# A hybrid encoder block on one core: the meta tokens' query steps moved to the front of each differential-attention unit, and the head of the output projection begun inside the last unit

## The reference

```
h    = rmsnorm(x);  proj = h @ w_in            # 3072 columns: NA q,k,v and diff q,k,v
na   = neighbourhood attention, 8 heads of 64
diff = differential attention, 4 heads: softmax(q1 k1) - lam * softmax(q2 k2), times v (128 wide)
diff = rmsnorm(diff over each head's 128) * subln * (1 - lambda_init)
x    = x + concat(na, diff) @ w_out
x    = x + expert_choice_ffn(rmsnorm(x))       # 16 experts, top-k tokens each
y    = rmsnorm(x), meta rows dropped
```

## Time and profile before

| | |
|---|---|
| median of 3 runs | 3216.51 us (3214.36 to 3216.98) |
| the profiled execution | 3214.47 us, of it span 3212.6 us |
| mean granted clock of TensorE | 0.954 |
| TensorE matmuls busy | 2997.2 us, 93% of the span |
| VectorE, ScalarE busy | 1873.7 us (58%), 1480.1 us (46%) |
| GpSimd busy | 170.8 us |

### The profile page before, as it was taken

The page is one execution under the profiler, slowest core; times in us unless marked ns, Lnnn a source line. Parts: engine busy times, 40 slices in busy tenths (PEclk is TensorE's granted clock), DMA queues, the critical chain, the costliest instruction groups (busy, mean ns, idle before and its releaser), DMA issues.

```text
span 3212.6 us, 49879 instructions
## 1 busy us (share of the span) xinstructions
PE 2997.2 (93%) x19549; PEld 2798.3 (87%) x19549; DVE 1873.7 (58%) x2996; ACT 1480.1 (46%) x2506; POOL 170.8 (5%) x177
## 2 busy tenths in 40 slices
PE   7999999898987896799999999999999999999993
PEld 7888887676854775799999999999999999999993
DVE  6232345564755236567667666766766766766672
ACT  4232323333333222456556555655655655555562
POOL 1000000000001000010110100010010011011001
PEclk9999999898988997899999999999999999999996
DMA  5322221100111333577777777777877777777774
GB/s 154 98 68 70 73 62 29 31 27 25 27 60 32 121 124 106 185 229 244 225 234 236 229 232 233 228 238 226 248 224 232 238 229 232 235 229 234 227 224 174
DMA packets 637872, 528.25 MB, mean 164 GB/s; under 512 B 30757, under 2 KB 618663, under 8 KB 637651
## 3 DMA queue, kind: packets, MB, share of 16 engines
q1 hardware_dynamic: 629458, 499.46, 50.1%
q0 software_dynamic: 8192, 25.70, 3.9%
HBM read 472.36 MB, written 40.79 MB: 160 GB/s over the span
## 4 chain that ended last, share of the span: by engine, by line
PE 74%; DVE 4%; ACT 2%; issue 2%; DMA 2%; POOL 1%; SPq 0%; ACTq 0%; POOLq 0%; DVEq 0%
PE ps L1840 38%; PE ps L1841 17%; PE ps L1759 5%; PE ps L1534 5%; PE ps L1729 2%; PE ps L1666 2%; ACT e_df L864 1%; PE ps L1885 1%; PE ps L1709 1%; DVE e_df L1243 1%; PE ps L1834 1%; PE ps L1727 1%; DMA wqkv<-w_in_dram 1%; DVE x L1306 0%; DVE mixT_lo L1293 0%
## 5 line engine op out<-in xcount | busy, mean ns | idle before, releaser
L1840 PE MATMUL ps<-xe,w_hi 128*128 128x392 f32 x4096 | 1196.1, 364 | 1.6 <-DVE xe L1440 1.6
L1841 PE MATMUL ps<-xe,w_lo 128*128 128x196 f32 x4096 | 1034.4, 253 | 0.0
L1427 DVE TENSOR_TENSOR w_lo<-raw,w_hi 128x2048 fp32r<-128x2048 f32 x384 | 875.5, 2284 | 0.2 <-issue 0.2
L1841 PEld LDWEIGHTS ps<-xe,w_lo 128*128 128x128 f32 x4096 | 784.4, 192 | 0.0
L1840 PEld LDWEIGHTS ps<-xe,w_hi 128*128 128x128 f32 x4096 | 770.4, 188 | 1.9 <-DVE xe L1440 1.9
L729 ACT ACTIVATE w_hi<-raw 128x2048 fp32r<-128x2048 f32 x384 | 731.9, 1911 | 10.1 <-DMA raw<-w_down_dram 9.9
L1840 PE MATMUL ps<-hid,w_hi 128*128 128x392 f32 x2048 | 609.4, 366 | 0.0
L1841 PE MATMUL ps<-hid,w_lo 128*128 128x196 f32 x2048 | 516.8, 252 | 0.0
L1841 PEld LDWEIGHTS ps<-hid,w_lo 128*128 128x128 f32 x2048 | 391.4, 191 | 0.0
L1840 PEld LDWEIGHTS ps<-hid,w_hi 128*128 128x128 f32 x2048 | 384.5, 188 | 0.0
L1460 DVE TENSOR_TENSOR gusum<-ps,part 128x392 f32<-128x392 f32 x256 | 145.0, 566 | 396.1 <-ACT part L729 396.1
(11 more groups left out here) (182 smaller groups left out, 3183.8 us busy)
## 6 DMA issues: line engine op xcount, KB each, us to landing
raw<-w_gate_dram SPq DMA_DIRECT2D x128, 1024.0 KB, 5.2
raw<-w_up_dram SPq DMA_DIRECT2D x128, 1024.0 KB, 5.2
raw<-w_down_dram SPq DMA_DIRECT2D x128, 1024.0 KB, 5.3
wqkv<-w_in_dram SPq DMA_DIRECT2D x24, 512.0 KB, 4.4
xt<-x_all_dram SPq DMA_DIRECT2D x12, 512.0 KB, 4.8
v_na<-v SPq DMA_DIRECT2D x64, 96.0 KB, 2.3
mixed_heads<-mix SPq DMA_DIRECT2D x96, 64.0 KB
mixs<-mixed_heads SPq DMA_DIRECT2D x12, 512.0 KB, 5.2
```

Source lines behind the costliest of these rows:

```text
L1427: dve.tensor_tensor(w_lo[:, n % NW, :], raw[:, n % NRAW, :], w_hi[:, n % NW, :].bitcast(f32), ALU.subtract).then_inc(lo_done, 1)
L1840: pe.matmul(out, w_hi[:, slot, cols], x.rearrange("p h n -> p (h n)"), start=first, stop=False)
L1841: return pe.matmul(out[:, 0:SLOTS], w_lo[:, slot, cols], x[:, 0, :], start=False, stop=last)
```

## The change

`diff_steps` now puts the two tail steps first in each unit. After them come the sample tiles and then the prompt tiles in units 0 to 2, and the prompt tiles and then the sample tiles in the last unit. The stores are numbered by step, and the two tail steps share a slot; the second's output waits for the first's square. ScalarE does the square of a step ahead of the exponentials instead of behind the copies.

In the last unit, SyncE issues the loads of T = 0 and T = 1 in steps 8 and 9 (`c_loads` waits by slot for the stores that it needs). VectorE makes the means of the tail tile and of tiles 0 to 3 in step 14 and the scaling of T = 0 and T = 1 in step 15, ahead of the last step's output; GpSimd does the power in three pieces (4, 16 and, after all squares, 32 columns). TensorE waits for all statistics (`df_m`) instead of all outputs before the first transposes of the output projection, and for all outputs before the first `h2_to_columns`. The SBUF places are rearranged so that the early tensors lie over the unused q0, k0 and the projection weights. The clearing of `aff` stays behind the last square.

```diff
-def diff_steps():
-    out = [(t, P, P, 0, PT) for t in range(PT)]
-    out += [(t, P, P, PT, FULL - PT) for t in range(PT, FULL)]
-    out += [(FULL, TAIL, TAIL, PT, FULL - PT), (FULL, TAIL, N_META, 0, PT)]
-    return out
+def diff_steps(last):
+    prompt = [(t, P, P, 0, PT) for t in range(PT)]
+    sample = [(t, P, P, PT, FULL - PT) for t in range(PT, FULL)]
+    tails = [(FULL, TAIL, TAIL, PT, FULL - PT), (FULL, TAIL, N_META, 0, PT)]
+    return tails + (prompt + sample if last else sample + prompt)
...
         mixs = R("mixs", [P, 2, D])
+        assert R.off <= late_off
+        R = Region(after_h)
         mixT_hi = R("mixT_hi", [P, 2, KD, P], f32r)
         mixT_lo = R("mixT_lo", [P, 2, KD, P], f32r)
         xr = R("xr", [P, 2, D])
+        assert R.off <= after_w
+        R = Region(late_off)
         x2 = R("x2", [P, 2, D])
...
-        def df_store(u, t):
-            return NT * UNITS + NT * u + t
+        def df_store(u, n):
+            return NT * UNITS + NT * u + max(n - 1, 0)
+        def stored_before(b, g):
+            return (g - b) // MIXR + 1
+        def last_store(T):
+            return df_store(UNITS - 1, [n for n, x in enumerate(DFS[-1]) if x[0] == c_tile(T)][-1])
...
+            def c_loads(T):
+                b, rows, row = T % 2, c_rows(T), c_tile(T) * P
+                if T >= 2:
+                    sp.wait_ge(mT_ready, T - 1)
+                for slot in range(MIXR):
+                    sp.wait_ge(mix_out[slot], 16 * stored_before(slot, last_store(T)))
+                sp.dma_start(mixs[0:rows, b, :], mix_d[row:row + rows, :]).then_inc(mixs_in[b], 16)
+                if T >= 2:
+                    sp.wait_ge(x2_ready, T - 1)
+                sp.dma_start(xr[0:rows, b, :], x_all[row:row + rows, :]).then_inc(xr_in[b], 16)
...
+                    if u == UNITS - 1 and s in (8, 9):
+                        c_loads(s - 8)
...
-            for b in range(MIXR):
-                sp.wait_ge(mix_out[b], 16 * stores(b))
             sp.wait_ge(df_sq, DS * UNITS + CREDIT)
-            for T in range(2):
-                c_loads(T)
...
+                    n = s - 3 - last
+                    if 0 <= n < DS:
+                        t, rows, keep, k0, kt = DFS[u][n]
+                        act.wait_ge(df_mix, u * DS + n + 1 + CREDIT)
+                        act.wait_ge(df_sq, u * DS + max(n - 1, 0) + CREDIT)
+                        apart(act)
+                        act.activation(e_sq[0:keep, n % 2, :], mix[0:keep, df_store(u, n) % MIXR, :], ACT.Square,
+                                       accum_out=ms_d[0:keep, t, u:u + 1]).then_inc(df_sq, 1)
                     if s < DS:
...
-                        if n == DS - 1:
+                        if n == 1:
                             dve.wait_ge(df_sq, u * DS + n + CREDIT)
...
+                    if last and s == DS:
+                        dve.wait_ge(df_sq, u * DS + FIRST + 2 + CREDIT)
+                        head_means(0, FIRST)
+                        head_means(FULL, NT).then_inc(sub_ms, 1)
+                    if last and s == DS + 1:
+                        for T in range(2):
+                            heads_scaled(T)
...
-            dve.tensor_scalar(ms_d[:, :, :], ms_d[:, :, :], 1.0 / (P * keep2), SUB_EPS / keep2, ALU.mult, ALU.add).then_inc(sub_ms, 1)
+            head_means(FIRST, FULL).then_inc(sub_ms, 1)
             own.mark(dve.memset(aff[:, :], -1.0))
             own.settle(dve)
-            dve.wait_ge(sub_rstd, 1)
...
             pe.wait_ge(wo_lo_done, KD)
-            pe.wait_ge(df_mix, DS * UNITS + CREDIT)
+            pe.wait_ge(df_m, 2 * DS * UNITS)
...
+                if T == 0:
+                    pe.wait_ge(df_mix, DS * UNITS + CREDIT)
                 pe.wait_ge(xn2_ready, T + 1)
...
             pool.wait_ge(sub_ms, 1)
-            rsqrt(rstd_d[:, :, :].rearrange("p t u -> p (t u)"), ms_d[:, :, :].rearrange("p t u -> p (t u)"),
-                  bcast(half_neg, 0, [[0, NT * UNITS]])).then_inc(sub_rstd, 1)
+            head_rstd(FULL, NT)
+            head_rstd(0, FIRST).then_inc(sub_rstd, 1)
+            pool.wait_ge(sub_ms, 2)
+            head_rstd(FIRST, FULL).then_inc(sub_rstd, 1)
```

More of the change, by code:

```diff
@@ L395, in build @@
         NA = na_steps()
-        DF = diff_steps()
-        NS, DS = len(NA), len(DF)
+        DFS = [diff_steps(u == UNITS - 1) for u in range(UNITS)]
+        NS, DS = len(NA), len(DFS[0])
         ITERS = 2 * UNITS
@@ L457, in build @@
         first_of = [min(s for s, x in enumerate(NA) if x[0] == ct) for ct in range(3)] + [NS]
-        def stores(slot):
-            total = df_store(UNITS - 1, NT - 1) + 1
-            return (total - slot + MIXR - 1) // MIXR
         PAIRS = FULL // 2
@@ L658, in _ @@
                         load_w(UNITS + u + 2, s // 4 - 1)
-                    if 0 <= s - 2 < DS and s - 2 != FULL:
-                        t, rows = DF[s - 2][:2]
-                        g = df_store(u, t)
+                    if 1 <= s - 2 < DS:
+                        t, rows = DFS[u][s - 2][:2]
+                        g = df_store(u, s - 2)
                         sp.wait_ge(df_mix, DS * u + s - 1 + CREDIT)
@@ L856, in _ @@
                         split_wq(UNITS + u + 2, s // 4 - 1)
+                    n = s - 3 - last
[6 more added lines that the diff above has]
+                                       accum_out=ms_d[0:keep, t, u:u + 1]).then_inc(df_sq, 1)
                     if s < DS:
-                        t, rows, keep, k0, kt = DF[s]
+                        t, rows, keep, k0, kt = DFS[u][s]
                         w = kt * P + N_META
@@ L868, in _ @@
                         n = s - 1
-                        t, rows, keep, k0, kt = DF[n]
+                        t, rows, keep, k0, kt = DFS[u][n]
                         act.wait_ge(df_t, u * DS + n + 1)
@@ L874, in _ @@
                              ps[:, 4 * BANK:5 * BANK].rearrange("p (j r) -> p j r", r=P)[:, :, 0:rows]).then_inc(df_et_a, 1)
-                    n = s - 3 - last
-                    if 0 <= n < DS:
-                        t, rows, keep, k0, kt = DF[n]
-                        act.wait_ge(df_mix, u * DS + n + 1 + CREDIT)
-                        act.wait_ge(df_sq, u * DS + max(n - 1, 0) + CREDIT)
-                        apart(act)
-                        act.activation(e_sq[0:keep, n % 2, :], mix[0:keep, df_store(u, t) % MIXR, :], ACT.Square,
-                                       accum_out=ms_d[0:keep, t, u:u + 1]).then_inc(df_sq, 1)
             act.wait_ge(df_sq, DS * UNITS + CREDIT)
@@ L1222, in _ @@
                     if 0 <= n < DS:
-                        t, rows, keep, k0, kt = DF[n]
-                        g = df_store(u, t)
+                        t, rows, keep, k0, kt = DFS[u][n]
+                        g = df_store(u, n)
                         dve.wait_ge(df_o, u * DS + n + 1)
@@ L1341, in prompt_rows @@
                 own.mark(dve.tensor_copy(aff[32:32 + N_EXP, 0:PART], aff_all[:, PART - N_META:N_PROMPT]))
-            for T in range(2):
-                heads_scaled(T)
             for T in range(2):
```

35 lines of the change are left out of this document (17 added, 18 removed).

## The result

| | kernel before | changed kernel |
|---|---|---|
| median | 3217.91 us (3214.36 to 3219.46, 6 runs) | 3204.61 us (3200.36 to 3207.07, 6 runs) |
| ratio to before | 1 | 0.9959, 95% interval 0.9946 to 0.9972 |
| profiled execution | 3214.47 us (span 3212.6, clock 0.954) | 3200.36 us (span 3198.6, clock 0.960) |

The changed kernel is 13.3 us faster by the medians; its median was forecast at 3206.0 us. On the second chip, beside other experiments, the same kernel gave 3206.44 us (3196.29 to 3210.48, 6 runs), ratio 0.9956 (0.9941 to 0.9970).

A forecast was written before the change was run, and what follows sets the result against it. TensorE was taken as the bound almost everywhere, with a GpSimd-dominated chain before the out-projection. Terms -12.4 - 0.5 + 3.4 = -9.5 gave 3205.0 from the profile, 3207 from the median; forecast 3206, range 3198.5 to 3213.

The forecast's parts named there:

- Part 1: Last combine to first out-projection matmul: early head statistics and power shorten it from 22.8 to 10.4 us, -12.4 us.
- Rival (a): GpSimd's power is cheap, both powers at the single-column price: chain 2.8 us shorter, 3203 us; chance 0.08.
- rival (e): Early head part does not start early, SyncE or VectorE being late: most of 12.4 lost, 3212 to 3217; chance 0.02.
- Part 2: Inside of the last unit, same steps in another order: net -0.5 us, anything from -2.5 to +1.5.
- Part 3: Ends of units 0 to 2, now holding prompt tiles: more TensorE idle, +1.1 us a unit, +3.4 in all.
- rival (b): Unit ends keep full clock speed and the out-projection starts at the upper level: 3195 to 3200 us; chance 0.10.
- (c): Unit ends cost more, lower clock covering longer weighted sums, 2 to 5 us a unit extra: 3212 to 3221; chance 0.19.
- (d): Slower: lower clock lasts through a unit's end into the next unit's covered steps, 3246 us; chance 0.04.
- The small edits: ScalarE's projection-weight waits, earlier square, second tail's mix and SBUF places: no change in time expected.

The follow-up runs named there:

- the runs above: Changed kernel with head statistics of one tile early instead of four, 3198.78 us (0.9945); and the changed kernel unedited, timed again, 3206.44 us (0.9956).
- the 44 columns: Late power in the changed kernel with one tile's head statistics early instead of four (44 columns late in place of 32); 3198.78 us, ratio 0.9945.
- The control: The changed kernel itself, no edit, timed again on another chip: 3206.44 us, ratio 0.9956 to the kernel before.

## Why the prediction was right

**Part 1, -12.4 forecast, -13.1 in the trace.** The chain was the one foretold. In GpSimd's groups by shape:

```profile
L1919 POOL TENSOR_TENSOR rstd_d<-ms_d,half_neg 128x32 f32<-128x32 f32 x1 | 5.4, 5413 | 2.4 <-DVE ms_d L1202 2.4
L1919 POOL TENSOR_TENSOR rstd_d<-ms_d,half_neg 128x16 f32<-128x16 f32 x1 | 2.9, 2913 | 0.0
L1919 POOL TENSOR_TENSOR rstd_d<-ms_d,half_neg 128x4 f32<-128x4 f32 x1 | 1.0, 1029 | 942.1 <-DVE ms_d L1202 942.1
```

The straight line through one and 52 columns gives 1.1, 3.0 and 5.5 us (the prediction says 5.4 for the last, a slip of its sum); 1.03, 2.91 and 5.41 were measured. The scaling was forecast at 6.6 us behind the start of the combine and came at 6.1: GpSimd started at 2.15 in place of 2.5, and its two operations took 3.90 in place of 4.1. From its end to the first matmul 2.3 us, forecast 2.5. One link was missing: the prediction let VectorE stand idle some 4 us before the scaling and nowhere else, and has one weighted sum behind the last combine. There are two, and VectorE waited 1.07 us for the first of them and 2.59 for the power. At the upper level the first hid beside GpSimd; at the lower one, in the runs above, the two are the chain. Rival (a), a power whose price hardly depends on the columns, is excluded by these rows and by the 44 columns at 7.37. The Trainium skill ("GPSIMD Engine Reference", section 3.1) prices a two-input elementwise operation, measured on an add, at 2.6 cycles an element behind a fixed dispatch. The trace doesn't agree with that for this power, which costs some 0.16 us for each column. The loads and SyncE were never waited for, so rival (e) is out. The late head alone undoes the gain: ratio 0.9999.

**Part 2, -0.5 forecast, +0.3.** From the last unit's first meta matmul to its last combine are 81.6 us after (1007.68 less 926.1) and 81.3 before (1007.04 less 925.7), inside the bounds. Both had 10.2 us at the lower level in that time. The control had 83.3 us, with 6.8 more at the lower level up to its last combine, so here the clock weighs more than the term.

**Part 3, +3.4 forecast, +0.6 and +3.1 in two executions.** The mechanism and the idle time were right: two waits for the copy per unit (2.99, forecast 3.3), none of 1.2 before the transposes, the six idle times of unit 2 together 9.36 (forecast 9.1 to 9.3), and the ends of all three units 3.3 us more idle than before. The clock, which I left as it was, is the mis-sized term: the time at the lower level fell from 70.8 to 57.3 and 63.0 us. In the first execution the matmuls of units 0 to 2 so took 2.3 us less and gave back most of the 2.9 that all idle time had grown. At the end of unit 2 the granted clock was 0.78 where it was 0.70. Why it stayed up longer isn't shown; the 2.99 us stand between longer runs of matmuls. This is rival (b), in a small share. Whether the new order costs or gains in the total is not settled: undone, it gave back 3.1 us of idle time at the ends and the ratio was still 0.0015 to 0.0018 higher; but with the head begun late it should have kept 4.5 us of the transition and the ratio kept nothing. Rivals (c) and (d), that the clock would cost more, did not come.

**The small edits.** ScalarE's waits for the projection weights in the differential stage, counted over the same stretch as in the earlier trace rows, became less: 25.0 us in four, the longest 6.7, in place of 28.3 with 8.1. TensorE's idle time at those places in units 0 and 1 is 8.0 us, 8.3 before: next to nothing, as forecast. In the run with the old order back it was 10.3 and with the tail steps last 6.7, so these places are not as indifferent to the order as the prediction had them.

**How near the number was** is in part luck. The terms sum to -9.5, and the medians moved by -13.3. From the median of the kernel before in six runs, 3217.91, they would have given 3208.4 in place of the measured 3204.61. The forecast was nearer because it went by the median of the first three, 1.4 us lower, and set 3206 between its two sums of 3205 and 3207. In the two profiles the terms miss by -0.7 (Part 1), +0.8 (Part 2) and -2.8 (Part 3, the clock), and -1.7 lie in stages that had no term. These are differences of single executions.

**The step that was too narrow** is another. The prediction took the ends of the units as given and priced only their change. They held a cost that neither kernel had touched and that I had named in passing ("which stands behind both exponentials"): its removal alone was worth 14.7 us, as much as the change. And it priced an idle microsecond as one microsecond. In the kernel before with the copy first, 3.4 us less idle time came with 10.7 us less in units 0 to 2, the other 7.3 by shorter matmuls at a higher granted clock.

Rival (b) also had the out-projection start at the upper level, 2.6 us. Its first 5.2 us ran at 0.62 in place of 0.50, the level having fallen 2.9 us before its first matmul, but the whole stage was no shorter (220.3 us, 219.4 before).

## What to carry to other kernels

Where an engine waits at a place that no other work covers, look at what stands ahead of the operation it waits for on that operation's own engine: the order can be changed for the last steps alone. Putting a copy ahead of two exponentials there brought as much as a rearranged stage. When a chain crosses GpSimd, price the operation by its columns and give it only those that are needed next, started before the last work that must precede it. Compare stage lengths of two kernels only beside two executions of one of them, with the granted clock next to each.

## What was not expected of the hardware

- Less idle time on TensorE gave back up to three times itself: -3.4 us idle and -17.4 us at the lower level made -10.7 us. It isn't a rule: with the sample steps last idle time fell by 8.6 us and the low time rose by 13.4. Both are differences of single executions.
- When the lower level falls inside a run differs between executions of one kernel: in the last unit with its head 13.2 us and 26.0 us, with equal idle time in units 0 to 2. What decides it stays open.
- At the lower level eight 128x128 matmuls of the weighted sum take 2.08 us against 1.16, and the eight transposes ahead of the out-projection 1.06 us against 0.68: 1.8 and 1.6 times.
